# FoX attention in a two-layer trunk: score maxima spread over the key tiles, splits in four steps, one turning of the maxima, output copied by ScalarE

## The reference

```python
q = _rmsnorm(q, q_norm); k = _rmsnorm(k, k_norm)
log_f = jax.nn.log_sigmoid((f_logit + b_f).astype(jnp.float32))
Ft = jnp.cumsum(log_f, axis=1).transpose(0, 2, 1)
...
    s = jnp.einsum("bqhd,bkhd->bhqk", qi, k, preferred_element_type=jnp.float32) * scale
    s = s + Fi[..., :, None] - Ft[:, :, None, :]
    s = jnp.where(kpos[None, :] <= qpos[:, None], s, -jnp.inf)
    p = jax.nn.softmax(s, axis=-1)
    return jnp.einsum("bhqk,bkhd->bqhd", p.astype(v.dtype), v)
```

## Time and profile before

| | us |
|---|---|
| runs (3) | 3717.51, 3721.48, 3736.63 |
| median | 3721.48 |
| the profiled execution | 3723.74 |
| its span in the profile | 3722.0 |
| TensorE busy | 3296.5 |
| VectorE busy | 1547.1 |
| ScalarE busy | 1009.8 |
| GpSimd busy | 542.1 |
| first FoX phase, first key tile to last sums | 297.1 |
| second FoX phase, the same | 307.0 |

### The profile page before, as it was taken

One profiled execution on the slowest core, in us unless ns is written; L12 is line 12 of the kernel. 1 busy time (PEld: TensorE's weight loads), 2 busy tenths in 40 slices (PEclk: granted clock), 3 DMA queues, 4 the chain that ended last, 5 costly groups with the idle time before them and its releaser, 6 DMA issues. The chain is left out here.

```text
span 3722.0 us, 62205 instructions
## 1 busy us (share of the span) xinstructions
PE 3296.5 (89%) x24708; PEld 2340.1 (63%) x24708; DVE 1547.1 (42%) x2258; ACT 1009.8 (27%) x1876; POOL 542.1 (15%) x304
## 2 busy tenths in 40 slices
PE   6979889999997688949979798999999976889499
PEld 4868767777773344437748686777777733444387
DVE  4136622222223555447441375222222235554475
ACT  4014322221222134323240143222122221343232
POOL 4100000000000122322241010000000001223222
PEclk9989999999997687969989899999999985789699
DMA  3225422222223300066332244222222133000663
GB/s 117 74 73 169 144 73 73 70 64 64 69 60 119 121 23 21 6 185 212 120 110 69 86 156 148 68 80 64 64 64 77 53 127 110 23 21 6 183 202 123
DMA packets 357723, 343.29 MB, mean 92 GB/s; under 512 B 95388, under 2 KB 290972, under 8 KB 353592
## 3 DMA queue, kind: packets, MB, share of 16 engines
q1 hardware_dynamic: 288520, 298.53, 25.4%
q10 hardware_dynamic: 68928, 40.93, 4.1%
HBM read 208.46 MB, written 130.91 MB: 91 GB/s over the span
## 5 line engine op out<-in xcount | busy, mean ns | idle before, releaser
L124 PE MATMUL rs_acc<-h_hi,rs_w_hi 128*128 128x512 f32 x1024 | 428.2, 418 | 0.0
L128 PE MATMUL rs_acc<-h_lo,rs_w_hi 128*128 128x512 f32 x1024 | 417.9, 408 | 0.0
L130 PE MATMUL rs_acc<-h_hi,rs_w_lo 128*128 128x512 f32 x1024 | 414.5, 405 | 0.0
L110 POOL TENSOR_TENSOR rs_w_lo<-rs_raw,rs_w_hi 128x1024 fp32r<-128x1024 f32 x32 | 76.3, 2384 | 1235.0 <-POOLq L109 1235.0
L1660 PE MATMUL so_acc<-so_wo_hi,so_m_hi 128*128 128x512 f32 x512 | 211.0, 412 | 42.8 <-POOL so_m_lo L1582 34.0
L124 PE MATMUL rp_acc<-h_hi,rp_w_hi 128*128 128x512 f32 x512 | 206.0, 402 | 41.6 <-PEq L121 41.6
L1372 ACT ACTIVATE fx_prob<-fx_ST 128x512 f32<-128x512 f32 (+3 forms) x320 | 157.0, 531 | 293.8 <-PE fx_ST L1242 155.6
L124 PEld LDWEIGHTS rs_acc<-h_hi,rs_w_hi 128*128 128x128 f32 x1024 | 192.3, 188 | 55.1 <-issue 16.5
L130 PEld LDWEIGHTS rs_acc<-h_hi,rs_w_lo 128*128 128x128 f32 x1024 | 192.6, 188 | 43.1
L128 PEld LDWEIGHTS rs_acc<-h_lo,rs_w_hi 128*128 128x128 f32 x1024 | 192.7, 188 | 36.7
L124 PE MATMUL pj_acc<-h_hi,pj_w_hi 128*128 128x512 f32 (+1 forms) x512 | 207.2, 405 | 5.2 <-PEq L121 5.2
(11 more groups left out here) (256 smaller groups left out, 6013.1 us busy)
## 6 DMA issues: line engine op xcount, KB each, us to landing
projT<-rs_stage SPq DMA_DIRECT2D x128, 256.0 KB, 2.1
pj_xb<-x SPq DMA_DIRECT2D x32, 512.0 KB, 3.3
projT<-rp_stage SPq DMA_DIRECT2D x64, 256.0 KB, 3.1
rs_raw<-w_in ACTq DMA_DIRECT2D x32, 512.0 KB
rs_nat<-rw SPq DMA_DIRECT2D x128, 128.0 KB, 2.4
so_stage<-x SPq DMA_DIRECT2D x64, 256.0 KB, 2.9
rp_pre<-projT SPq DMA_DIRECT2D x16, 899.5 KB, 8.2
projT<-pj_stage SPq DMA_DIRECT2D x56, 256.0 KB, 2.0
```

The lines of the kernel that those rows point to most:

```text
L110: self.nc.gpsimd.tensor_tensor(self.w_lo[q][:, :, 0:m], self.raw[:, :, 0:m], self.w_hi[q][:, :, 0:m].bitcast(F32), ALU.subtract).then_inc( ...
L124: ins = M(acc, self.w_hi[q][:, k, 0:m], self.h_hi[:, k, cols], start=(k == 0), stop=False)
L128: M(acc, self.w_hi[q][:, k, 0:m], self.h_lo[:, k, cols], start=False, stop=False)
L130: ins = M(acc, self.w_lo[q][:, k, 0:m], self.h_hi[:, k, cols], start=False, stop=(k == KC - 1))
```

## The change

`plan()` builds one list of everything that is done beside the key tiles (splits, maxima, minima, values) over all rounds, and takes from it up to a goal that grows with the number of key tiles done: 7 tiles of maxima ahead of the first key tile, then 3 more for each 2 key tiles up to the 24th, then 19 for each 20, and at least a whole next round's by its second-last key tile. "r" is four entries (0 and 1: rounded parts of a head by ScalarE, 0 also GpSimd's copies; 2 and 3: remainders of a head by VectorE, 2 also ScalarE's second copy of the keys, under a semaphore `k_split`), placed before the last four tiles of maxima of the round before. "l" comes one key tile after its minimum, "o" after key tile 0 and "u" after key tile 2. The turning puts both heads into one set of four transposes (rows 64 to 66 and 32 to 34 of `LT`). ScalarE instead of VectorE copies `O` to `yo`. `prob` has four buffers.

Counting entries, the order is: before key tile 0 of round 0 s0.0 to s1.2; all four steps of round 2's splits between key tiles 1 and 2 of round 0, all of round 3's between 5 and 6 of round 1, round 4's between 7 and 10 of round 2, round 5's from there to tile 2 of round 3, round 6's and 7's one per key tile. The turnings of rounds 2, 3, 4, 5, 6, 7 come after key tiles 6 of round 1, 10 of round 2, 2 and 10 of round 3, 3 of round 5 and 10 of round 6; those of rounds 3, 4, 5 and 6 have the transposes of v and one tile of maxima right ahead of them, and that of round 4 also the sums of round 2 ahead of those. The last tile of maxima is done by key tile 9 of round 6.

```diff
-        NP = 3
+        NP = 4
-        LS = P.sb("LS", [128, 2 * QT, KX])
+        LS = P.sb("LS", [128, QT, KX])
...
+            beside = [("r", 0, i) for i in range(4)] + [("v", 0, 0)]
             for R in range(NR):
+                n = len(stat[R % NQ])
+                for i in range(n):
+                    if R + 1 < NR and i >= n - 4:
+                        beside.append(("r", R + 1, i - n + 4))
+                    beside.append(("s", R, i))
+                beside.append(("x", R, 0))
                 if R + 1 < NR:
+                    beside.append(("v", R + 1, 0))
...
+            def ahead(goal):
+                nonlocal done, ns
+                while done < len(beside) and (ns < goal or beside[done][0] == "x"):
+                    order.append(beside[done])
+                    ns += beside[done][0] == "s"
+                    if beside[done][0] == "x":
+                        turns.append((nm + 1, ("l", beside[done][1], 0)))
+                    done += 1
...
+            ahead(len(stat[0]))
+            turned(1)
+            ahead(len(stat[0]) + 3)
+            for R in range(NR):
+                for j in range(keys[R % NQ]):
+                    turned(nm)
                     order.append(("m", R, j))
-                    if R > 0 and j == 1:
+                    nm += 1
+                    if R > 0 and j == 0:
                         order.append(("o", R - 1, 0))
-                    if R > 0 and j == 3:
+                    if R > 0 and j == 2:
                         order.append(("u", R - 1, 0))
...
+                    goal = len(stat[0]) + 3 + min(nm, 24) * 3 // 2 + max(0, nm - 24) * 19 // 20
+                    for r in range(1, NR):
+                        if nm >= sum(keys[i % NQ] for i in range(r)) - 2:
+                            goal = max(goal, sum(len(stat[i % NQ]) for i in range(r + 1)))
+                    ahead(min(total, goal))
...
                 if k == "l":
                     pe.wait_ge(s["x_rdy"], R + 1)
-                    for h in two:
-                        pe.wait_ge(s["lt_free"], lt_n[k, R, h] - 1)
-                        for j in range(QT):
-                            ins = Tr(LT[0:KX, j * 128:(j + 1) * 128], LS[:, QT * h + j, :], ident[:])
-                        ins.then_inc(s["lt_rdy"], 1)
+                    pe.wait_ge(s["lt_free"], lt_n[k, R] - 1)
+                    for j in range(QT):
+                        ins = Tr(LT[0:KX, j * 128:(j + 1) * 128], LS[:, j, :], ident[:])
+                    ins.then_inc(s["lt_rdy"], 1)
...
-                if k == "r":
-                    c = slice(Q * TB, (Q + 1) * TB)
+                if k == "r" and x > 1:
+                    c, h = slice(Q * TB, (Q + 1) * TB), x - 2
                     v.wait_ge(s["a_split"], R + 1)
...
-                    v.wait_ge(s["pv_done"], last[R])
-                    if R > 1:
-                        v.wait_ge(yo_st[R % 2], 16 * (R // 2))
-                    V.tensor_copy(yo[:, R % 2], O[:]).then_inc(s["o_free"], 1)
                 if k == "u":
                     v.wait_ge(s["rl_rdy"], R + 1)
-                    v.drain()
+                    v.wait_ge(s["o_free"], R + 1)
...
+                    A(Q2[p][x][0:HD, c], rq[x][:, R % 2], ACT.Copy)
+                    ins = A(K2[p][x][0:HD, c], rk[x][:, R % 2], ACT.Copy)
+                    if x == 1:
+                        act.drain().then_inc(s["a_split"], 1)
+                if k == "r" and x == 2:
                     for h in two:
-                        A(Q2[p][h][0:HD, c], rq[h][:, R % 2], ACT.Copy)
-                        A(K2[p][h][0:HD, c], rk[h][:, R % 2], ACT.Copy)
+                        ins = A(K1[p][h][0:HD, c], rk[h][:, R % 2], ACT.Copy)
+                    ins.then_inc(s["k_split"], 1)
...
+                    for h in two:
+                        a = (HD, HD // 2)[h]
+                        ins = A(Q2[p][h][HD:KX, c], LT[a:a + 3, :], ACT.Copy)
+                    ins.then_inc(s["lt_free"], 1)
                     act.drain().then_inc(s["l_rdy"], 1)
+                if k == "o":
+                    act.wait_ge(s["pv_done"], last[R])
+                    if R > 1:
+                        act.wait_ge(yo_st[R % 2], 16 * (R // 2))
+                    A(yo[:, R % 2], O[:], ACT.Copy).then_inc(s["o_free"], 1)
```

More of the change, by code:

```diff
@@ L1061, in phase_fox @@
         O, LT = P.ps("O", [128, TB]), P.ps("LT", [128, TB])
[L1062 removed]
+        names = ("c_in", "c_rdy", "a_split", "k_split", "d_split", "p_split", "s_rdy", "m_rdy", "x_rdy",
                  "lt_rdy", "lt_free", "l_rdy", "v_rdy", "t_rdy", "p_rdy", "pv_done", "add_d", "add_p", "rl_rdy", "o_free", "rl_free", "yo_rdy")
@@ new lines, in plan @@
+            turns, order, done, ns, nm = [], [], 0, 0, 0
+            total = sum(len(stat[R % NQ]) for R in range(NR))
+            def ahead(goal):
[6 more added lines that the diff above has]
+                    done += 1
@@ L1088, in plan, with turned @@
+            def turned(now):
+                while turns and turns[0][0] <= now:
+                    order.append(turns.pop(0)[1])
+            ahead(len(stat[0]))
[4 more added lines that the diff above has]
+                    turned(nm)
                     order.append(("m", R, j))
-                    if R > 0 and j == 1:
+                    nm += 1
+                    if R > 0 and j == 0:
                         order.append(("o", R - 1, 0))
-                    if R > 0 and j == 3:
+                    if R > 0 and j == 2:
@@ L1103, in phase_fox @@
         for k, R, x in order:
-            for h in (two if k == "l" else (0,) if k in "vu" else ()):
-                lt_n[k, R, h] = len(lt_n) + 1
+            if k in "lvu":
+                lt_n[k, R] = len(lt_n) + 1
         tiles = [(R, j) for R in range(NR) for j in range(keys[R % NQ])]
@@ L1130, in _ @@
                 if R > 1:
-                    sp.wait_ge(s["a_split"], R - 1)
+                    sp.wait_ge(s["k_split"], R - 1)
                     sp.wait_ge(s["d_split"], R - 1)
@@ L1161, in _ @@
                 p, Q = R // NQ, R % NQ
-                if k == "r":
+                if k == "r" and x == 0:
                     pool.wait_ge(raw_in[R % 2], 96 * (R // 2 + 1))
@@ L1290, in _ @@
                 p, Q = R // NQ, R % NQ
-                if k == "r":
-                    c = slice(Q * TB, (Q + 1) * TB)
+                if k == "r" and x > 1:
+                    c, h = slice(Q * TB, (Q + 1) * TB), x - 2
                     v.wait_ge(s["a_split"], R + 1)
[L1294 to L1297, removed]
+                    V.tensor_tensor(Q1[p][h][0:HD, c], rq[h][:, R % 2], Q2[p][h][0:HD, c].bitcast(F32), ALU.subtract)
+                    ins = V.tensor_tensor(K1[p][h][HD:128, c], rk[h][:, R % 2], K2[p][h][0:HD, c].bitcast(F32), ALU.subtract)
+                    if h == 1:
+                        ins.then_inc(s["d_split"], 1)
                 if k == "v":
-                    v.wait_ge(s["lt_rdy"], lt_n[k, R, 0])
+                    v.wait_ge(s["lt_rdy"], lt_n[k, R])
                     V.tensor_copy(vs[p][:, QT * Q:QT * Q + QT, :], LT[:].rearrange("p (j c) -> p j c", j=QT)).then_inc(s["lt_free"], 1)
@@ L1347, in _ @@
                 c = slice(Q * TB, (Q + 1) * TB)
-                if k == "r":
+                if k == "r" and x < 2:
                     act.wait_ge(raw_in[R % 2], 96 * (R // 2 + 1))
```

34 lines of the change are left out of this document (14 added, 20 removed).

## The result

The changed kernel takes 3695.3 us (median of 9 runs, 3686.2 to 3703.2) against 3721.5 us of the kernel before (9 runs): ratio 0.9932, 95% interval 0.9915 to 0.9949. That is 26 us faster, outside the forecast range of 3595 to 3688 and a third of the 80 us forecast. The sign and the place were right, the size was not.

A forecast was written before the change was run, and what follows sets the result against it. TensorE, busy 89% of the span, loses idle time and half clock in the two FoX phases; 17 us per phase of idle and transposes plus 21 and 27 of clock sum to 82, taken as 80: 3642 us, range 3595 to 3688.

The forecast's parts named there:

- The copy by ScalarE: Output copy O to yo: TensorE's 9.3 us of waits per phase go to none, at no cost to ScalarE.
- One turning: Transposes of the maxima through LT: 5.9 us of waits and 3 us of transposes per phase removed.
- Splits in steps, and the eased second half: VectorE's splits and maxima: large gaps go, leaving 3 us idle in round 0, 3.5 in round 1; eased from round 2's end.
- The queue on LT: Turnings waiting for v's copy in the LT bank: 8.9 us of new waits per phase beyond round 2's 3.5.
- a sign of being wrong: TensorE idle for LT above 12 us, listed among the signs that would show the forecast wrong.
- Idle in all: TensorE's idle time per FoX phase: from 36 us to 21.4, a gain of 14.
- The clock: Half-clock time of TensorE falls to 50 us per phase from 101 and 117, gaining 21 and 27 us.
- Smaller, new waits take the place of the old: Late VectorE holds v's copy in rounds 1 and 2; only rounds from 3 on gain, 20 us per phase, 3682; chance 0.12.
- Rival 4: FoX phases: nothing but the copy and the turning pays, 9 us per phase, 3703 us; chance 0.05.
- Deeper: The clock rises already in round 0, only each phase's head at half clock: 38 us more in both, 3604; chance 0.17.
- The clock of the clean rounds: Key tiles mixed with maxima run rounds 3 to 6 at half clock: 36 us slower per phase, 3794; chance 0.04.

The follow-up runs named there:

- e1_turn_later: The changed kernel with the turnings of rounds 2 to 7 one key tile later and each round's last maxima one key tile earlier; 3657.5 us, ratio 0.9832.
- e6_later_and_behind: The changed kernel with the turnings of rounds 2 to 7 one key tile later and each round's v behind four of its maxima; 3627.3 us, ratio 0.9761.
- e9_late_minimum: e6_later_and_behind with ten needless reduces on VectorE ahead of the minimum of each of rounds 2 to 7; 3682.1 us.
- e4_old_order: The changed kernel without the new order of plan(): four split steps in a row, output copy and sums one key tile later; 3679.4 us, ratio 0.9889.
- e2_narrow_maxima: The changed kernel with VectorE's maxima over the first 128 columns only and exponentials scaled by 0.001, part of the maxima left out; 3612.9 us, one run.

## Why the prediction was wrong

*The copy by ScalarE*: 9.3 us of waits to none, as forecast. Alone, part of it comes back before the maxima.

*One turning*: about 9 us a phase forecast, 24 us of the whole time measured alone (17 to 33 by its interval), with the clock 0.01 higher. Right.

*Splits in steps, and the eased second half*: the three large gaps of the earlier trace rows before maxima are gone, and what waits for maxima is 4.8 us, less than the 9 that I had left (3 in round 0 and 6 of small waits). The round-0 gap of 3 us isn't there; no gap of the head is longer than 1.00 us. I erred on the safe side.

*The queue on LT*: 12.4 us forecast before the turnings of rounds 2 to 6, 14.9 measured (3.5, 2.5, 2.3, 0.5, 3.6 forecast; 2.36, 2.92, 1.16, 3.03, 5.39 measured), and 3.4 more before those of rounds 7 (2.41) and 1 (1.00), forecast at nothing: 18.3 in all, above the 12 that I had written as a sign of being wrong. Rounds 2 and 4 were priced too high. Ahead of the turnings of rounds 5, 6 and 7 VectorE had instructions that took up to 2.1 us longer beside GpSimd's adds (an add of 3.28 us, the subtraction of 2.75, an add of 3.29), which I knew from the earlier trace rows and put into a rival instead of the sum.

*Idle in all*: 14 us of gain forecast per phase, 10.3 and 9.8 measured. So far the sum holds in the main.

*The clock*: this is the step that failed. I had written that after 1331 the clock holds, with one fall for round 1's gap and chance falls, 50 us of half clock in all, worth 21 and 27 us. The changed kernel has 27.5 us of head at half clock (35 forecast, right enough: it rises at 1313) and 81 us in six later stretches, 109 us where the kernel before had 101 and 117. Put into the term as I wrote it, that is (101 - 109) x 0.9 x 0.45 = -3 us in the first phase and (117 - 109) x 0.9 x 0.45 = 3 us in the second: nothing in all. In the same text stood four waits of 2.3 to 3.6 us and one of 0.5 before turnings, and the sentence that such a gap is followed by a long stretch at half clock. I priced these waits at their own length and gave the clock's term as if they weren't there; e1_turn_later and e6_later_and_behind took them away and the clock rose to 0.87 and 0.91, e9_late_minimum put them back and it fell to 0.86 and 0.83. With the clock's term at nothing the sum is 17 + 17, 3688, and the idle time that came out about 4 us a phase short of its forecast makes up the rest. The new order would have appeared as what it is, neutral or worse until the turnings are moved (16 us worse than the old order with the same parts, by e4_old_order).

The reading of the rows behind that sentence was loose too. The two longest stretches at half clock, which I put behind the large gaps, began before them: at 1290.6, where the gap of 3.71 us runs from 1295.2 to 1299.0, and at 1437.3, where that of 2.79 us runs from 1444.6 to 1447.4. Of the four gaps of the earlier trace rows it is those of 2.40 and 3.23 us that a fall goes with, at 1358.9 for 3.4 us and at 1464.7 for 17.

*The rivals*: "Smaller, new waits take the place of the old" named the mechanism, a late VectorE that holds v's copy and so the turning, but had it in rounds 1 and 2 and let the rounds from 3 on gain; the waits stand mostly in those. Its 3682 is short by the clock, which was left out of it too. Rival 4 (nothing but copy and turning pays, 3703) lies nearer to the 3695.3 by number, but by a sum without the clock: these two parts with the old order give 3679. "Deeper" failed with the main forecast, and its working was unsound: it takes the 34 us of the head as gained while its words leave the head at half clock, by which it would be about 3619, not 3604. "The clock of the clean rounds" was refuted by e2_narrow_maxima and e6_later_and_behind. What it feared did happen to round 3, by another mechanism. These are the windows of its sixteen key tiles, in the kernel before and in the changed one:

```profile
1391.20:1432.00 40.80, 38.51 (x172) 17.37 (x173) 18.54 (x20) 21.49 (x43) 16.61 (x10) 1.00 0.09 27
```
```profile
1387.90:1453.60 65.70, 60.72 (x205) 28.91 (x204) 34.45 (x38) 24.20 (x46) 16.92 (x10) 0.71 0.06 17
```

It went from 41 us, all at 1.0, to 66 us with more maxima in it, of which 38 ran at 0.5, in the stretches up to 1402.0, from 1405.4 to 1419.2 and from 1436.4 to 1446.4.

*What stays open*: how firmly a single fall is tied to a single gap, and why the low stretches last as long as they do. Counted over both FoX windows of all thirteen traces of this study, 61 of 62 gaps of 2 us or more that began at full clock had a fall within 5 us of their start, but also 48 of 83 gaps of 1 to 2 us and 41 of 173 of 0.5 to 1 us, where a moment picked at random at full clock has one in about 1 of 7 cases; and 10 of 139 falls had no gap above 0.5 us in the 5 us ahead of them. So a gap of 2 us or more has a fall with it nearly always, and not every fall has such a gap. In the changed kernel the low stretches last 10 to 20 us with TensorE busy nearly throughout; in e4_old_order there are nine of them in the first phase, five under 4 us long, although its idle time is 35.7 us, more than the change's. What ends them was not tried.

## What to carry to other kernels

Where TensorE's clock moves, price a wait by the fall of the clock that comes with it: here gaps of 2.5 to 5.1 us, put back by needless work of VectorE, cost 2.4 times their length in all. When work is spread evenly, look next at the entries that close a chain across engines (here minimum, turning, copy, through one shared PSUM bank): they need a key tile of distance from what they wait for, and moving two such entries was worth 68 us, where the rewrite of the order without that had been worth less than nothing. Equal idle time isn't equal time: about three quarters of the gaps of 0.5 to 1 us left the clock up, and all but one of those of 2 us or more had a fall with them.

## What the runs showed of the hardware that was not expected

A subtraction of 64x512 on VectorE takes 0.685 us in the median of both kernels; its longest was 1.00 us before and 2.76 us after, when the steps were spread to where GpSimd adds:

```profile
L1321 DVE TENSOR_TENSOR fx_ka<-fx_rk,fx_kb x32: 684/685/2755, 1269.9 to 3321.7; 64x512 fp32r<-64x512 f32 x32
```

The instruction of 2.75 us began 0.16 us after GpSimd's of 2.37 us did (1475.11 and 1474.95, above) and ended 0.55 us after it. It is not alone: in the changed kernel 30 instructions of VectorE with two inputs in SBUF, subtractions and adds of 128x1024, began inside an add of GpSimd, anywhere from 0.16 to 2.19 us into it. Each of the six subtractions ended 0.55 us after that add and each of the 24 adds of 128x1024 1.08 us after it. The 24 maxima that began inside one, which read PSUM, took no longer than elsewhere (1.23 us at most). The Trainium skill (SBUF — State Buffer, "SBUF: two separate sides") has it that VectorE, in an instruction with two SBUF inputs, and a GpSimd instruction that reads SBUF take a shared pair of ports by exclusive lock, so that the later one waits for the whole instruction of the other; by that the subtraction would end about its own 0.68 us after GpSimd's, and the add its 1.22 us, and the trace has 0.55 and 1.08. No run here took GpSimd's adds away, so that what they cost in all wasn't measured. In a chain that TensorE waits for, a two-input instruction of VectorE can thus cost what is left of a GpSimd instruction more.
